# Trunk with top-2-of-8 experts: the expert order computed ahead of the first gather, the last norm's squares ahead of the overflow jump, the last normalise and its stores in column halves

## The chip, the core and the metric

The kernel runs on one core of one Trainium2 chip. TensorE multiplies into PSUM, VectorE (DVE in the rows) and ScalarE (ACT) work between PSUM and SBUF, GpSimd (POOL) builds masks and loads a few small tensors, SyncE (SP) issues nearly all transfers. Each engine takes its own instructions in their order and waits at semaphores for the others. The metric is the device time of one execution in microseconds; lower is better.

## What is computed

A two-layer trunk over 256 frames of width 1024, all in float32. Layer 0 has a spatial-gating and a gated-DeltaNet mixer and a dense SwiGLU. Layer 1 has stick-breaking attention and then the part that the change touches: a router picks two of eight experts for each frame, and every expert is a SwiGLU of inner width 2816. At the end stands one RMSNorm.

```python
def moe_swiglu(xn, w_router, w1, w3, w2):
    logits = (xf @ w_router).astype(jnp.float32)
    vals, idx = lax.top_k(logits, TOP_K)
    gates = jax.nn.softmax(vals, axis=-1)
    combine = jnp.sum(jax.nn.one_hot(idx, N_EXPERTS, dtype=jnp.float32) * gates[..., None], axis=1)
    y = jnp.zeros_like(xf)
    for e in range(N_EXPERTS):
        y = y + combine[:, e:e + 1].astype(xf.dtype) * swiglu(xf, w1[e], w3[e], w2[e])
...
    return rmsnorm(h, final_norm)
```

## The kernel before

The frames lie in two tiles of 128 (index `t`); `h` [128, 2, 1024] is the residual. The line numbers here and in the rows are those of the kernel before.

**Experts.** Expert 0 comes first; the other seven are taken in an order that is found while the kernel runs, by how many frames each got. Slots 0, 2, 4, 6 of that order are "big": their frames (up to 128) are multiplied with weights that are split in a high part (`all_hi`, ScalarE, L883) and a low part (`low`, VectorE, L1904), three matmuls for each product (L620 to L622). Slots 1, 3, 5, 7 are "small": up to 64 frames, full float32 matmuls straight from the loaded weights (L1717 up, L1738 down). What doesn't fit those capacities goes to "overflow items", a loop behind the eight slots that is jumped over when there are none (`n_more` is 0).

**Steps and pieces.** The matmuls of the experts are a list `STEPS`: phase up 0 (slot 0, first half of the inner width, 16 steps of 9 matmuls), up 1 (slot 1, 16 steps), down 0, up 2 (second half of slot 0), down 1, and so on, always two phases of a big slot around those of small ones. The weights come in `PIECES` of 704 KB (up) or 1 MB (down) into one ring in SBUF, `room`. `place_pieces` gives each piece its place and what must have been used before it may be overwritten. Pieces 0 to 15 are those of up 0 and are loaded before the router has decided anything. Pieces 16 to 19 (slot 1) take places that the dense layers' last units held, and piece 20 + k takes a place that step k of up 0 has used. SP issues the pieces in their order (L695) and, ahead of piece 16, waits for `order_ready` and reads the expert's number from `order_i` (L702).

**Router and order on VectorE.** After the top-2 (L2211 to L2228) VectorE writes the table `nat` (place, gate and count for each expert), then `sel_p` (L2239), with which TensorE gathers slot 0's frames (L1661), then `sel_w` (L2246, `places_back(0)`), which is needed for slot 0's way back much later. It splits the gathered frames (`xg_lo`, L2322), and the order is worked out between the splits of up 0: `compare_counts` (L2272 to L2276) at step 0, `rank_experts` (L2280 to L2283) at step 1, `order_table` (L2288 to L2292) at step 2, whose last instruction casts the order into `order_i`.

**The end.** The last slot's result goes back by four matmul groups (L1698), and VectorE adds each to `h` (L2369, four instructions: two column halves of tile 0, then two of tile 1). Each engine then reads `n_more` from `item_i` (TENSOR_LOAD) and jumps over the overflow loop. Behind its jump VectorE raises `h_ready` (drain, L2479), ScalarE loads the exp and ln table (L1195) and does the last norm's squares, ln and exp for each tile (L846 to L848, `inverse_rms(4)`), VectorE multiplies (L1876, one instruction of 1024 columns for each tile), and SP stores each tile with one transfer of 512 KB (L727).

## Time and profile before

| what | value |
|---|---|
| time, median of 3 runs | 1207.49 us (1205.4 to 1207.52) |
| time of the profiled execution | 1207.14 us, of which its span is 1205.3 us |
| TensorE busy | 1149.9 us (95%) |
| VectorE busy | 669.2 us (56%) |
| ScalarE busy | 562.7 us (47%) |
| GpSimd busy | 49.6 us (4%) |
| mean granted TensorE clock | 0.988 |
| transfers | 351.08 MB, mean 291 GB/s |

The span is the time from the first to the last instruction; 1.84 us lie around it. Of the chain of work that ended last, 88% is TensorE. The experts' part begins at about 519 us of the span and its last matmul ends at 1193.66 us; the eight experts hold 276.8 MB of weights.

### The profile page before, as it was taken

To read this page: it belongs to the slowest core of one execution; us is meant where nothing else is said; L and a number is where in the kernel's file an instruction comes from. 1 tells how busy PE (TensorE), PEld (TensorE's weight loads), DVE (VectorE), ACT (ScalarE), POOL (GpSimd) and SP (SyncE) were. 2 spreads that over 40 slices of the span, in tenths; PEclk is the share of its full clock that TensorE was granted. 3 is DMA by queue.
4 is the path that set the end of the run, shared out by engine and by line. 5 is a ranking of instruction groups with operands and counts; after the bars stand their busy time and mean duration, and the time that the engine had idled before them with its cause. 6 is when DMAs were issued, how large, how long until landed. Compare 5 with 4: busy or idle time off the path is not lost.

```text
span 1205.3 us, 16293 instructions
## 1 busy us (share of the span) xinstructions
PE 1149.9 (95%) x6555; PEld 852.7 (71%) x6555; DVE 669.2 (56%) x740; ACT 562.7 (47%) x642; POOL 49.6 (4%) x93
## 2 busy tenths in 40 slices
PE   5989899999999999899999999999999999999995
PEld 5979778888879976685486688648658468387351
DVE  4875664544455523582384788427578058574143
ACT  4772355344444476452363677226447056263131
POOL 8010000000000022000000000000000000000000
PEclk9999999999999999999999999999999999999998
DMA  9632059755325822139999999999999999999992
GB/s 319 184 116 72 29 169 369 238 175 187 128 70 177 330 74 72 66 139 416 413 415 410 413 415 412 400 414 414 411 414 415 415 412 412 413 413 415 413 407 78
DMA packets 116737, 351.08 MB, mean 291 GB/s; under 512 B 8136, under 2 KB 55280, under 8 KB 116656
## 3 DMA queue, kind: packets, MB, share of 16 engines
q1 hardware_dynamic: 115552, 347.11, 74.8%
q0 software_dynamic: 1104, 2.86, 0.8%
q8 instruction: 54, 0.88, 0.3%
q14 instruction: 27, 0.22, 0.1%
HBM read 348.89 MB, written 1.05 MB: 290 GB/s over the span
## 4 chain that ended last, share of the span: by engine, by line
PE 88%; DVE 4%; ACT 2%; DMA 2%; POOL 2%; issue 1%; POOLq 0%; DVEq 0%; ACTq 0%
PE ps L620 20%; PE ps L621 19%; PE ps L622 19%; PE ps L1717 11%; PE ps L1738 7%; PE ps L1661 3%; DMA room<-in_o_moe_w_dram 2%; PE ps L1673 1%; PE ps L1370 1%; DVE low L1904 1%; POOL level L741 1%; PE ps L1578 1%; PE ps L1590 1%; DMA gam<-in_e_sgu_w_dram 1%; PE ps L1698 1%
## 5 line engine op out<-in xcount | busy, mean ns | idle before, releaser
L1904 DVE TENSOR_TENSOR low<-room,all_hi 128x1408 fp32r<-128x1408 f32 (+1 forms) x216 | 308.0, 1458 | 202.6 <-ACT all_hi L883 202.0
L883 ACT ACTIVATE all_hi<-room 128x1408 fp32r<-128x1408 f32 (+1 forms) x216 | 265.3, 1255 | 258.6 <-DMA room<-in_o_moe_w_dram 177.4
L1717 PE MATMUL ps<-room,xg_raw 128*64 128x512 f32 (+1 forms) x768 | 152.5, 558 | 0.0
L620 PE MATMUL ps<-all_hi,xg_hi 128*128 128x512 f32 (+1 forms) x384 | 144.8, 377 | 2.0 <-DVE low L1904 1.0
L621 PE MATMUL ps<-low,xg_hi 128*128 128x512 f32 (+1 forms) x384 | 144.6, 376 | 0.0
L622 PE MATMUL ps<-all_hi,xg_lo 128*128 128x512 f32 (+1 forms) x384 | 144.0, 375 | 0.0
L620 PE MATMUL ps<-all_hi,x_hi 128*128 128x512 f32 (+1 forms) x336 | 125.1, 372 | 5.1 <-ACT xn L972 2.4
L621 PE MATMUL ps<-dense_lo,x_hi 128*128 128x512 f32 (+1 forms) x336 | 122.8, 366 | 0.0
L622 PE MATMUL ps<-all_hi,x_lo 128*128 128x512 f32 (+1 forms) x336 | 122.5, 365 | 0.0
L1717 PEld LDWEIGHTS ps<-room,xg_raw 128*64 128x64 f32 x768 | 54.6, 137 | 95.5 <-issue 95.4
L1897 DVE TENSOR_TENSOR dense_lo<-slots_a,all_hi 128x2048 fp32r<-128x2048 f32 x40 | 91.4, 2290 | 47.5 <-ACT all_hi L876 47.5
L876 ACT ACTIVATE all_hi<-slots_a 128x2048 fp32r<-128x2048 f32 x40 | 76.7, 1918 | 40.7 <-PE ps L622 37.1
L620 PE MATMUL ps<-x_hi,all_hi 128*128 128x256 f32 x288 | 83.0, 288 | 4.4 <-DVE x_lo L1890 3.4
L1738 PE MATMUL ps<-room,m_raw 128*64 128x512 f32 x352 | 83.2, 610 | 2.3 <-DVE y_lo L2359 2.3
L620 PEld LDWEIGHTS ps<-all_hi,xg_hi 128*128 128x128 f32 x384 | 72.1, 188 | 16.9 <-issue 3.5
L1897 DVE TENSOR_TENSOR dense_lo<-slots_c,all_hi 128x2048 fp32r<-128x2048 f32 x25 | 57.3, 2293 | 46.6 <-ACT all_hi L876 46.5
L621 PE MATMUL ps<-x_lo,all_hi 128*128 128x256 f32 x288 | 81.8, 284 | 0.0
L622 PE MATMUL ps<-x_hi,dense_lo 128*128 128x256 f32 x288 | 81.2, 282 | 0.0
L622 PEld LDWEIGHTS ps<-all_hi,xg_lo 128*128 128x128 f32 x384 | 72.1, 188 | 11.5
L621 PEld LDWEIGHTS ps<-low,xg_hi 128*128 128x128 f32 x384 | 72.1, 188 | 11.4
L620 PEld LDWEIGHTS ps<-all_hi,x_hi 128*128 128x128 f32 x336 | 64.1, 191 | 18.6 <-issue 5.5
L620 PE MATMUL ps<-all_hi,m_hi 128*128 128x512 f32 x176 | 71.6, 407 | 2.2 <-DVE m_lo L2342 2.2
(363 smaller groups left out, 1566.9 us busy)
## 6 DMA issues: line engine op xcount, KB each, us to landing
room<-in_o_moe_w_dram SPq DMA_DIRECT2D x256, 704.0 KB, 15.6
room<-in_o_moe_w_dram SPq DMA_DIRECT2D x80, 1024.0 KB, 18.2
slots_c<-in_e_ffn_w_dram SPq DMA_DIRECT2D x36, 512.0 KB, 6.8
slots_a<-in_e_ffn_w_dram SPq DMA_DIRECT2D x30, 512.0 KB, 5.3
slots_a<-in_e_w_in_dram SPq DMA_DIRECT2D x24, 512.0 KB, 8.7
slots_a<-in_o_w_qkv_dram SPq DMA_DIRECT2D x18, 512.0 KB, 4.5
room<-in_o_moe_w_dram SPq DMA_DIRECT2D x16, 512.0 KB, 17.1
slots_a<-in_e_w_out_dram SPq DMA_DIRECT2D x8, 512.0 KB, 4.0
```

Source lines behind the costliest of these rows:

```text
L620: pe.matmul(o, a_hi, b_hi, start=first, stop=False)
L621: pe.matmul(o, a_hi, b_lo, start=False, stop=False)
L622: return pe.matmul(o, a_lo, b_hi, start=False, stop=last)
L741: after(pool.affine_select(out=t, in_=t, pattern=pattern, compare_op=op, fill=fill, base=base, channel_multiplier=cm))
L876: act.activation(w_hi[i % SPLITS][:, :], ring[slot][:, :], ACT.Copy).then_inc(hi_done, 1)
L883: act.activation(unit_hi(st), raw_of(v, off, st.size), ACT.Copy).then_inc(hi_done, 1)
L1370: last = mm(ps[rows, bank, m * CH:(m + 1) * CH], a(u, rows), b(u, rows), start=True, stop=True)
L1661: last = mm(ps[:, gather_bank(q, c // 4), at:at + n], xn[:, t, c * P:(c + 1) * P], sel_p[:, t, 0:n], start=(t == 0), stop=(t == TILES - 1))
L1717: last = mm(ps[a * SMALL:(a + 1) * SMALL, o + b, 0:n], xg_raw[:, c, :], raw[a][:, c0:c0 + n], start=(c == 0), stop=(c == DC - 1))
L1738: last = mm(ps[hf * SMALL:(hf + 1) * SMALL, y_bank(st.q), :], m_raw[st.n % 2][:, j, st.a * SMALL:(st.a + 1) * SMALL], raw[:, hf * 512:(hf ...
L1897: tt(w_lo[i % SPLITS][:, :], ring[slot][:, :], w_hi[i % SPLITS][:, :].bitcast(F32), ALU.subtract).then_inc(lo_done, 1)
L1904: tt(unit_lo(st), raw_of(v, off, st.size), unit_hi(st).bitcast(F32), ALU.subtract).then_inc(lo_done, 1)
```

## The change

- `order_experts` is new: it works out only the order (one row of 49 products, a sum, a cast into `order_i`) and raises `order_ready`. `compare_counts`, `rank_experts` and `order_experts` now stand in front of `gathered(0)`, and `places_back(0)` behind it. `order_table` stays at step 2 without its cast.
- The last norm's squares, ln and exp (`last_rms`) stand on ScalarE in front of its read of `n_more` and its jump; they wait for the adds of each tile (`scat_added`) and write the squares into a tile of their own. If there are overflow items, they are done again behind them (`more_added`, `more_normed`).
- VectorE reads `n_more` ahead of the last slot's four adds, jumps behind them, has no drain on the path without items, and normalises each tile in two column halves; SP stores each half (256 KB) as it is ready.

```diff
+                act.wait_ge(scat_added, 4 * (NE - 1) + 2 * (t + 1))
+                last_rms(t, rinv_ready)
...
             with act.If(n_more > 0):
...
-            act.preload_act_table_set(EXP_LN)
-            inverse_rms(4)
...
-            places_back(0)
...
-                vec.tensor_copy(order_i[0:1, :], tab[0:1, 6, 0:NE]).then_inc(order_ready, 1)
...
+            def order_experts():
+
+                after(tt(ids_moved, nat[0:1, 6, 1:NE].unsqueeze(1).to_broadcast([1, R7, R7]), rank4[0:1, 3], ALU.mult))
+                after(vec.tensor_reduce(ids_order[:, 1:NE], ids_moved, AX.X, ALU.add))
+                vec.tensor_copy(order_i[0:1, 1:NE], ids_order[:, 1:NE]).then_inc(order_ready, 1)
+
+            compare_counts()
+            rank_experts()
+            order_experts()
             gathered(0)
+            places_back(0)
...
-                    if st.j == 0:
-                        compare_counts()
-                    if st.j == 1:
-                        rank_experts()
...
             finished(NE - 1)
+            vec.wait_ge(items_ready, 1)
+            n_more = vec.value_load(item_i[0:1, 0, 0:1], min_val=0, max_val=7)
             add_out(NE - 1)
...
-            vec.wait_ge(items_ready, 1)
-            n_more = vec.value_load(item_i[0:1, 0, 0:1], min_val=0, max_val=7)
             with vec.If(n_more > 0):
...
-            vec.wait_ge(items_ready, 1)
-            vec.drain().then_inc(h_ready, 2 * TILES)
+                vec.drain().then_inc(more_added, 1)
+                vec.wait_ge(more_normed, TILES)
+            vec.wait_ge(ld_gain, 48)
             for t in range(TILES):
-                normalise(4, t)
+                vec.wait_ge(rinv_ready, TILES * 4 + t + 1)
+                for hf in range(2):
+                    cs = slice(hf * 512, (hf + 1) * 512)
+                    stt(xn[:, t, cs], h[:, t, cs], stat[:, 4, 4 + t:5 + t], gain[:, 0, cs], ALU.mult, ALU.mult)\
+                        .then_inc(out_ready, 1)
```

**VectorE at the first gather, before.** `low8960` is the low part of up 0's step 2 and `low10368` that of step 3; a name's first number is its place in `room`.

```order
L2246 TENSOR_SCALAR sel_w_56<-iota,nat_50 128x128 [waits vec_own]
...
L2322 TENSOR_TENSOR xg_lo_62<-ps,xg_hi_61 128x512 [waits xgh_ready] x2
L1904 TENSOR_TENSOR low8960_7327<-room_49,all_hi 128x1408 [waits hi_done]
L2272 TENSOR_TENSOR router_tmp_58<-nat_50 128x49 [waits counts_read]
...
L1904 TENSOR_TENSOR low10368_7338<-room_49,all_hi 128x1408 [waits hi_done,vec_own]
...
L2283 TENSOR_TENSOR router_tmp_58<-router_tmp_58 128x49 [waits vec_own]
...
L2290 TENSOR_REDUCE tab_51<-router_tmp_58 128x56 [waits vec_own]
L2291 COPY tab_51<-nat_50 128x8
L2292 CAST order_i_54<-tab_51 1x8 [waits vec_own]
L1904 TENSOR_TENSOR low14592_7371<-room_49,all_hi 128x1408 [waits hi_done]
```

**The same place after the change.**

```order
L2301 TENSOR_TENSOR router_tmp_58<-router_tmp_58 128x49 [waits vec_own]
L2390 TENSOR_TENSOR router_tmp_58<-nat_50,router_tmp_58 1x49 [waits vec_own]
L2391 TENSOR_REDUCE router_tmp_58<-router_tmp_58 1x7 [waits vec_own]
L2392 CAST order_i_54<-router_tmp_58 1x7 [waits vec_own]
L2339 TENSOR_TENSOR xg_lo_63<-ps,xg_hi_62 128x512 [waits xgh_ready] x2
L2266 TENSOR_SCALAR sel_w_56<-iota,nat_50 128x128 x2
L1924 TENSOR_TENSOR low8960_7343<-room_49,all_hi 128x1408 [waits hi_done]
...
L2308 TENSOR_REDUCE tab_51<-router_tmp_58 128x8x7 [waits vec_own]
L2309 COPY tab_51<-nat_50 128x8
L1924 TENSOR_TENSOR low14592_7387<-room_49,all_hi 128x1408 [waits hi_done,vec_own]
```

The order's cast now stands ahead of the wait for the gathered frames instead of behind the fourth split of up 0, `sel_w` stands behind that wait, and the nine instructions of `compare_counts` and `rank_experts` are gone from between the splits.

**ScalarE behind the last slot's result, after the change** (before, the read of `item_i` stood right behind the copy to `y_small`, and the table load and the squares, which waited for `h_ready`, behind the jump).

```order
L1156 ACTIVATE y_small_75<-ps 64x512 [waits raw_used]
L1186 ACT_TABLE_LOAD
L1182 ACTIVATE squares_59,stat<-h 128x1024 [waits scat_added]
L1183 ACTIVATE stat<-stat,const 128x1 [waits act_own]
L1184 ACTIVATE stat<-stat 128x1 [waits act_own]
L1182 ACTIVATE squares_59,stat<-h 128x1024 [waits scat_added]
...
L1204 TENSOR_LOAD item_i_53 [waits items_ready]
L1204 ISA x2
L1205 COMPARE_AND_BRANCH
```

The six activations no longer have a jump, of ScalarE's or of VectorE's, ahead of them.

## Rows read from the trace of the kernel before

**Rows 1.** Waits of SP's queue, 519 to 600 us: total us, times, longest.

```profile
SPq L702 <- DVE order_i L2292: 34.1, 1, 34.1
```

**Rows 2.** Busy us of each engine by stretch, granted clock, DMA share, GB/s.

```profile
554.40:594.20 39.80, 39.79 (x204) 14.63 (x203) 3.73 (x6) 2.87 (x4) 0.00 (x0) 1.00 1.02 415
594.20:603.30 9.10, 6.91 (x30) 5.69 (x30) 9.10 (x11) 8.52 (x12) 0.00 (x0) 0.81 1.02 410
...
770.00:780.00 10.00, 10.00 (x50) 4.22 (x51) 0.00 (x0) 0.00 (x0) 0.00 (x0) 1.00 0.98 375
780.00:1160.00 380.00, 378.92 (x1862) 243.74 (x1859) 207.58 (x196) 169.83 (x175) 0.00 (x0) 1.00 1.02 413
```

**Rows 3.** Timeline of VectorE around the first gather: start us, us, instruction.

```profile
514.94 0.60 DVE L2246 TENSOR_SCALAR sel_w<-iota,nat 128x128 f32<-128x128 f32 x2
517.79 0.69 DVE L2322 TENSOR_TENSOR xg_lo<-ps,xg_hi 128x512 fp32r<-128x512 f32 x1 [2.25 <-ACT xg_hi L1120]
...
520.54 1.62 DVE L1904 TENSOR_TENSOR low<-room,all_hi 128x1408 fp32r<-128x1408 f32 x1
522.07 0.20 DVE L2272 TENSOR_TENSOR router_tmp<-nat 128x49 f32<-128x49 f32 x1
...
525.85 0.20 DVE L2280 TENSOR_TENSOR router_tmp<-router_tmp 128x49 f32<-128x49 f32 x1
...
526.57 0.21 DVE L2283 TENSOR_TENSOR router_tmp<-router_tmp 128x49 f32<-128x49 f32 x1
...
528.36 0.56 DVE L2288 TENSOR_TENSOR router_tmp<-nat,router_tmp 128x392 f32<-128x392 f32 x1
...
529.63 0.16 DVE L2292 CAST order_i<-tab 1x8 int32<-1x8 f32 x1
```

**Rows 4.** Timeline of TensorE, the first matmul of up 0's step 6.

```profile
531.37 0.50 PE L620 MATMUL ps<-all_hi,xg_hi 128*128 128x512 f32 x1 [0.57 <-DVE low L1904]
```

**Rows 5.** The chain that ended last, from up 1 to down 0.

```profile
572.35 20.05 DMA room<-in_o_moe_w_dram
...
592.42 1.07 ACT all_hi L883
...
596.39 0.80 PE ps L620
597.19 0.43 PE ps L621
...
599.75 0.26 PE ps L621
```

**Rows 6.** Timeline of ScalarE ahead of slot 6's down phase.

```profile
1139.22 2.01 ACT L883 ACTIVATE all_hi<-room 128x1024 fp32r<-128x1024 f32 x2 [41.20 <-DMA room<-in_o_moe_w_dram]
```

**Rows 7.** The chain over the experts' part, at that down phase.

```profile
1143.91 0.43 PE ps L620
```

**Rows 8.** The chain at the end; DVEq is VectorE's sequencer.

```profile
1192.82 1.39 DVE h L2369 x2
...
1194.61 0.07 DVEq L2467
...
1197.46 0.02 DVEq L2478
...
1197.57 1.16 ACT xn L846 x2
...
1199.08 0.20 ACT stat L848
...
1200.92 1.28 DVE xn L1876
```

**Rows 9.** ScalarE's read of `item_i`: ns, first and last start.

```profile
L1187 ACTq TENSOR_LOAD <-item_i x1: 462/462/462, 1190.8 to 1190.8; - x1
```

**Rows 10.** Timeline of ScalarE behind that read.

```profile
1192.03 1.28 ACT L1195 ACT_TABLE_LOAD   x1 [0.61 <-issue]
```

**Rows 11.** DMA share in 40 slices of 0.1 us, 1202 to 1206 us.

```profile
DMA  9899899820499899899999930000000000000000
```

More of the change, by code:

```diff
@@ L421, in trunk @@
         router_tmp = over(gain_at + 4 * D)[0]("router_tmp", [P, D])
+        squares = over(gain_at + 4 * D)[0]("squares", [P, D])
         y_hi = over(gain_at + 4 * D)[0]("y_hi", [SLOTS, D], F32R)
@@ L1172, in _, with last_rms @@
             finished(NE - 1)
+            def last_rms(t, ready):
+                after(act.activation(squares[:, :], h[:, t, :], ACT.Square, accum_out=stat[:, 4, t:t + 1]))
+                after(act.activation(stat[:, 4, 2 + t:3 + t], stat[:, 4, t:t + 1], ACT.Ln, scale=1.0 / D, bias=eps_col))
+                act.activation(stat[:, 4, 4 + t:5 + t], stat[:, 4, 2 + t:3 + t], ACT.Exp, scale=-0.5).then_inc(ready, 1)
+            act.preload_act_table_set(EXP_LN)
+            for t in range(TILES):
+                act.wait_ge(scat_added, 4 * (NE - 1) + 2 * (t + 1))
+                last_rms(t, rinv_ready)
             def evac_y(n):
@@ L1189, in _ @@
                 used(act, A_ITEM - 1)
+                act.preload_act_table(ACT.Silu)
                 with act.Fori(0, n_more) as it:
```

27 lines of the change are left out of this document (18 added, 9 removed).

## Prediction

> **What bounds the kernel now.** I read the waits of SP's queue first. For the order of the experts it stands still for 34.1 us [rows 1], until the cast that ends at 529.79 us [rows 3]; after that the transfers never rest. The busy times by stretch come next: from there on the DMA share is 1.01 to 1.03 at some 413 GB/s, and TensorE is busy all the time too, 378.92 of 380 us between 780 and 1160 us [rows 2]. Two full resources don't bind alike, so the waits decide. TensorE has nearly no idle time behind 603 us, while the transfers run short once: 375 instead of 413 GB/s between 770 and 780 us, 0.9 us of their time, where the next piece waited for a place that TensorE had yet to use. So the experts' part is bound by TensorE, and the transfers are a close second. Then I looked for the places where TensorE does wait. There are three that the change could touch. At step 6 of up 0 it waits 0.57 us for VectorE's low part [rows 4]. Between up 1 (busy until 594.2 us, 39.79 of 39.80 us [rows 2]) and down 0 (first matmul at 596.39 us [rows 5]) it waits 2.2 us, and the chain goes back over ScalarE's split to a transfer that lands at 592.4 us: data that came late because the order did. And at the end everything hangs on a string of single steps [rows 8].
>
> **The change, part by part, at the start.** `compare_counts` takes the place that `sel_w` had at 514.94 us and lasts 0.6 us (its five instructions begin at 522.07 us and are through when the next one can start), `rank_experts` 0.95 us (four, first and last in rows 3), `order_experts` three links of the same kind, 0.65 us. The order is ready at 514.94 + 0.6 + 0.95 + 0.65 = 517.15 us, 12.6 us before 529.79 us. That is 0.6 us ahead of VectorE's wait for the gathered frames, which ends at 517.79 us, so this cover hides it; each 0.1 us beyond would delay the gather's low parts and up 0 by as much.
>
> What it costs later: `sel_w` (0.6 us) now stands between `xg_lo` and the low part of step 2, which began at 520.54 us. That one would begin at 521.1 us and end at 522.7 us; TensorE starts step 0 at about 519.0 us by my estimate, a step being 4224 columns at the 0.24 us for 512 that the matmuls take at the full clock (0.26 us with its tail in rows 5), 1.94 us, so step 2 starts at 522.9 us. Cost between 0 and 0.3 us, taken as 0. Before step 6's low part VectorE loses 0.6 + 0.95 + 0.2 us (the cast) and gains 0.6 us of `sel_w`: it is 1.1 us earlier, more than the wait of 0.57 us. Gain 0.6 us (0 to 0.7).
>
> Do the transfers really come earlier? Pieces 16 to 19 need nothing of up 0; they are 4 x 0.721 MB / 413 GB/s = 7.0 us of transfer. Piece 20 + k needs step k, and the steps free one each 1.94 us where a piece takes 1.75 us, and stop for slot 1's gather. So the lead when up 0 ends lies between 7.0 and 12.6 us, and I take 9. Up 1 frees two pieces a step and holds nobody up. The piece of the 592.4 us needs to come 2.2 + 0.6 us earlier and comes 9 earlier; down 0's splits and `m_lo` then lie wholly beside up 1's matmuls, in which VectorE and ScalarE are nearly idle (3.73 and 2.87 us of 39.80 [rows 2]). The wait of 2.2 us goes.
>
> With it goes its echo. Behind the wait the granted clock of the stretch is 0.81 [rows 2]: matmuls take 0.43 us, the lower of the two levels (1.2 GHz), from 596.39 to 599.75 us, and then 0.26 us [rows 5]. 3.36 us of work at half speed are 1.6 us lost (1.5 to 1.7). Without the gap TensorE runs on at 2.4 GHz. Sum of the start: 0.6 + 2.2 + 1.6 = 4.4 us.
>
> **Is it kept until the end?** TensorE has no slack behind it, so a shift stays a shift if its data come as early. At 770 us the transfers already wait for TensorE; with 9 us of lead against 4.4 us they wait there longer, and from that place both run as before, only 4.4 us earlier. How thin that is: ahead of slot 6's down phase the data come at 1139.22 us [rows 6]; with one high part (1.0 us) and one low part (1.2 us) they are ready at 1141.5 us, for matmuls that start at 1143.91 us [rows 7]. The margin is 2.4 us.
>
> **The end.** Tile 0's adds are through at 1194.21 us; its squares began at 1197.57 us and would begin at 1194.26 us. Squares to exp took 1.71 us for tile 0 and 3.31 us for both [rows 8], so the scales are there at 1195.97 and 1197.57 us; the adds of tile 1 end at 1195.53 us, in time for the second squares. The table load, 1.28 us [rows 10], falls between the copy and the adds.
>
> VectorE's jump stays behind the adds. Its branch stood at 1194.61 us and its next instruction at 1197.46 us [rows 8]: 2.85 us. The read in front of it, 0.46 us for ScalarE [rows 9] and some 0.3 us around it, is now hidden ahead of the adds, so VectorE gets through at 1196.65 us. The change moves the read, not the jump: this and no longer ScalarE would be late next. Bounds: a jump that must wait for the last add to end, 1195.53 + 2.85 = 1198.4 us; or one as cheap as ScalarE's, whose read, jump and all cost 0.61 us of idle time [rows 10], and then the scales decide. Four halves of 1.28 / 2 = 0.65 us end at 1199.25 us instead of 1202.20 us: gain 2.95 us (1.2 to 3.3). I take the middle one since it is this engine's own jump.
>
> The Trainium skill ("Runtime: NRT & Kernel Launch", Instruction fetch mechanics) says that a taken branch whose target isn't in the pages already fetched stalls for a fetch. That fits VectorE's dear jump and ScalarE's cheap one; since VectorE's jump spans the same loop as before, it would stay dear by that rule too, and a lucky page would give the 3.3 us.
>
> The last store's data take 1.4 us, from slice 10 to slice 23 [rows 11]; a half takes 0.65 us less, if rows of 2 KB move as fast as rows of 4 KB (0 to 0.65 us; taken 0.65). Sum of the end: 3.6 us (1.2 to 4.0).
>
> **Sum.** 4.4 + 3.6 = 8.0 us: 1207.14 - 8.0 = 1199.1 us, 0.35 us more against the median of the runs. I say 1199.3 us; the bounds alone give 1198.6 to 1202.1 us.
>
> **Rivals.** *The lead is taken back*: the transfers don't keep up behind 780 us, and TensorE keeps only its margin of 2.4 us. For it: a DMA share of 1.02 throughout. Against it: the gap at 770 us. 1207.14 - 2.4 - 3.6 = 1201.1 us. *The transfers are the bound after all*: then all 12.6 us come through, 1191 us; against it stands TensorE without waits. *The order brings nothing*: the second expert's pieces wait for room, not for the order; only the end is left, 1203.5 us. The 34.1 us of rows 1 speak against it.
>
> *The stores run one after another.* Between the last multiply's end (1202.20 us) and the end of the span lie 3.1 us, 1.4 of them data, so 1.7 us are fixed. Four halves in a row are 4 x 2.35 = 9.4 us from 1197.3 us, 5.1 us more than in the forecast: 1204.2 us. The second store's packets follow the first's within 0.2 us [rows 11], which speaks against it. The Trainium skill ("DMA: Bandwidth & Descriptors", Rules for kernel authors) asks for 1 MB or more in a transfer, which is the rule against the halves.
>
> *Slower:* transfers that are ahead get issued one by one as places come free, and each then shows its fixed time. With 1.7 us on each of up 0's 16 pieces they lose 27 us, are 14 us late instead of 12.6 early, and TensorE waits for about that long: 1217 us. It decides where fewer than two transfers are under way. When they did run short, at 770 us, it cost 0.9 us.
>
> **Chances.** Forecast 0.70, lead taken back 0.13, order brings nothing 0.06, transfers the bound 0.05, stores in a row 0.03, slower 0.03. A measurement of this kernel can tell about 0.2% (2.4 us) from no change. All but the last are faster by more than that; with the stores' case close to it I give 0.94 faster, 0.03 within, 0.03 slower. The range holds the first two cases, the bounds and the spread of 2.1 us between the runs of before: 1196.8 to 1203.0 us.
>
> **What would show it.** The cast into `order_i` near 517 us and the transfers 12.6 us earlier; no wait at step 6; down 0's first matmul right behind up 1, at a granted clock of 1.00; the last expert matmul 4.4 us earlier; the first squares right behind tile 0's adds; VectorE idle until 2.4 us behind them. I am wrong if TensorE waits for data behind 603 us, or if VectorE's jump lasts otherwise.

## The result, and where the 7 us came from

The changed kernel takes 1200.44 us (median of 4 runs, 1199.14 to 1201.01), the kernel before in the same rounds 1207.51 us (4 runs, 1205.4 to 1208.23). The ratio is 0.9943, 95% interval 0.9926 to 0.996: 7.1 us less, 8.0 were forecast, and the forecast of 1199.3 us is 1.1 us short. The profiled execution took 1201.01 us with a span of 1199.3 us; against the profiled execution of before (1207.14 and 1205.3 us) that is 6.0 us of span, and these are accounted for below, from the front of the program to its end. Lines behind the first few hundred stand 4 to 28 lines further down than before: L625 to L627 are the three matmuls of a split product, L1737 and L1758 the small slots' up and down matmuls.

**The order.** Timeline of VectorE in the changed kernel (start us, us, instruction), to hold against [rows 3]:

```profile
516.78 0.16 DVE L2392 CAST order_i<-router_tmp 1x7 int32<-1x7 f32 x1
517.58 0.69 DVE L2339 TENSOR_TENSOR xg_lo<-ps,xg_hi 128x512 fp32r<-128x512 f32 x1 [0.64 <-ACT xg_hi L1126]
```

and the waits of SP's queue there (total us, times, longest), to hold against [rows 1]:

```profile
SPq L707 <- DVE order_i L2392: 21.4, 1, 21.4
```

The cast ends at 516.94 us (forecast 517.15) and SP waits 12.7 us less (forecast 12.6). The idle 0.64 us in front of `xg_lo` is still there: the cover held, the gather's low part waited for ScalarE and not for the order.

**The busy times by stretch** (length, busy us of TensorE's matmuls and weight loads, VectorE, ScalarE, GpSimd, granted clock, DMA share, GB/s), to hold against [rows 2]:

```profile
554.40:592.90 38.50, 38.50 (x201) 14.19 (x195) 7.17 (x9) 7.55 (x11) 0.00 (x0) 1.00 1.01 404
592.90:602.00 9.10, 9.10 (x46) 7.47 (x45) 8.14 (x9) 7.07 (x10) 0.00 (x0) 1.00 1.02 415
750.00:760.00 10.00, 10.00 (x64) 8.81 (x63) 9.90 (x14) 5.25 (x9) 0.00 (x0) 1.00 0.89 347
760.00:770.00 10.00, 10.00 (x47) 6.62 (x47) 1.61 (x3) 0.00 (x0) 0.00 (x0) 1.00 0.88 304
770.00:780.00 10.00, 10.00 (x54) 3.61 (x52) 0.00 (x0) 0.00 (x0) 0.00 (x0) 1.00 1.00 391
780.00:1160.00 380.00, 375.64 (x1841) 242.59 (x1839) 208.98 (x200) 170.28 (x177) 0.00 (x0) 1.00 1.02 413
```

TensorE works without a break around 593 us, where it had waited 2.2 us, and the granted clock is 1.00 in place of 0.81. The chain at the same place (start us, us, what; compare [rows 5]):

```profile
571.73 21.41 PE ps L1737 x108
593.14 0.43 PE ps L625
593.57 0.23 PE ps L626
```

No transfer is in it any more: down 0 comes right behind up 1. Its first matmul starts 3.3 us earlier than in [rows 5]; 0.2 us of that lay already ahead of up 0, 0.8 are the wait of step 6 [rows 4] and what hung on it, 2.3 the wait ahead of down 0. The matmuls then run at 0.23 us where those of [rows 5] ran at 0.43 until 599.75 us, so that at slot 0's turn the lead is 4.8 us. TensorE keeps nearly all of it for 540 us (4.5 us at slot 6's down phase).

**Where the lead was spent.** The transfers give their 12.7 us back in two stretches. The first lies beside the end of up 0 (the same columns as above; the changed kernel, then the kernel before):

```profile
540.00:570.00 30.00, 30.00 (x149) 17.60 (x149) 8.52 (x10) 7.01 (x9) 0.00 (x0) 1.00 0.94 353
```

```profile
540.00:570.00 30.00, 30.00 (x154) 18.30 (x155) 9.50 (x11) 7.10 (x9) 0.00 (x0) 1.00 1.02 417
```

353 GB/s instead of 417 for 30 us are 4.6 us of lead: up 0's steps free the places no faster, as the forecast said when it took 9 us for the lead behind up 0. Between 750 and 780 us they run at 347, 304 and 391 GB/s instead of 413: (66 + 109 + 22) GB/s times 10 us over 413 GB/s, 4.8 us more, of which the kernel before loses 0.9 too. That was forecast for 770 us (the transfers wait for places that TensorE has yet to use); it began 20 us earlier and took more, because the lead was greater. 12.7 - 4.6 - 3.9 = 4.2 us are left, about TensorE's own lead. Behind it the margin was to be 2.4 us at slot 6's down phase. In this execution it was not there. ScalarE's timeline (start us, us, instruction), to hold against [rows 6], and the waits of TensorE:

```profile
1136.85 2.01 ACT L889 ACTIVATE all_hi<-room 128x1024 fp32r<-128x1024 f32 x2 [43.55 <-DMA room<-in_o_moe_w_dram]
1139.40 2.02 ACT L889 ACTIVATE all_hi<-room 128x1024 fp32r<-128x1024 f32 x2 [0.55 <-DMA room<-in_o_moe_w_dram]
...
PE ps L1693 <- DVE u_act L2349: 0.9, 1, 0.9
```

In the kernel before the first pair of high parts starts at 1139.22 us [rows 6] and the second at

```profile
1141.78 2.01 ACT L883 ACTIVATE all_hi<-room 128x1024 fp32r<-128x1024 f32 x2 [0.55 <-DMA room<-in_o_moe_w_dram]
```

The data of both pairs come 2.4 us earlier in the changed kernel, while TensorE comes 4.5 us earlier: 2.1 us of the 2.4 us of margin are gone. ScalarE's split of the late piece then stands in front of `u_act`, and TensorE waits for that (0.9 us, and some tenths around it). 3.5 us of lead are left when the last slot's matmuls end.

**The end.** The chain of the changed kernel (start us, us, what), to hold against [rows 8]:

```profile
1189.25 0.97 DVE h L2386 x2
...
1190.56 1.40 DVE h L2386 x2
1191.96 1.14 issue
1193.11 0.02 DVEq L2505
...
1193.18 1.42 DVE xn L2508 x2
```

and ScalarE beside it:

```profile
1190.68 1.06 ACT L1182 ACTIVATE squares<-h 128x1024 f32<-128x1024 f32 x1 [1.53 <-DVE h L2386]
...
1192.19 0.20 ACT L1184 ACTIVATE stat<-stat 128x1 f32<-128x1 f32 x1
```

The first scale is there at 1192.39 us, but VectorE starts to multiply at 1193.18 us. Its own jump is what is late next, as forecast: the instruction behind the jump comes 1.15 us behind the last add, where 1196.65 against 1195.53 us, that is 1.12, was worked out. From the first add to the end of the span it takes 10.06 us, in the kernel before 12.48 us: 2.4 us gained. 3.5 and 2.4 us make the 6.0 us of the span. The forecast had 4.4 and 3.6.

### The profile page after: what moved, and what is told of

It reads as the page before. It is cut to its first block, busy times and chain, and to the rows that moved or that the text cites. A ratio compares the mean times of both kernels' runs of the same rounds, so it can differ in the third digit from the quotient of the medians.

```text
span 1199.3 us, 16296 instructions
## 1 busy us (share of the span) xinstructions
PE 1148.1 (96%) x6555; PEld 851.9 (71%) x6555; DVE 669.4 (56%) x744; ACT 561.9 (47%) x642; POOL 49.5 (4%) x93
## 4 chain that ended last, share of the span: by engine, by line
PE 89%; DVE 4%; DMA 2%; ACT 2%; POOL 2%; issue 1%; POOLq 0%; DVEq 0%; ACTq 0%; SPq 0%
PE ps L625 20%; PE ps L626 20%; PE ps L627 20%; PE ps L1737 11%; PE ps L1758 7%; PE ps L1681 3%; DMA room<-in_o_moe_w_dram 2%; PE ps L1693 1%; PE ps L1390 1%; POOL level L747 1%; PE ps L1598 1%; PE ps L1610 1%; DMA gam<-in_e_sgu_w_dram 1%; PE ps L1718 1%; PE ps L1715 1%
## 5 line engine op out<-in xcount | busy, mean ns | idle before, releaser
L1737 PE MATMUL ps<-room,xg_raw 128*64 128x512 f32 (+1 forms) x768 | 152.5, 558 | 0.0
L625 PE MATMUL ps<-all_hi,xg_hi 128*128 128x512 f32 (+1 forms) x384 | 145.0, 378 | 1.4 <-DVE y_small L2378 1.0
L627 PE MATMUL ps<-all_hi,xg_lo 128*128 128x512 f32 (+1 forms) x384 | 144.2, 375 | 0.0
L625 PE MATMUL ps<-all_hi,x_hi 128*128 128x512 f32 (+1 forms) x336 | 125.2, 373 | 5.1 <-ACT xn L978 2.4
L627 PE MATMUL ps<-all_hi,x_lo 128*128 128x512 f32 (+1 forms) x336 | 122.6, 365 | 0.0
L1737 PEld LDWEIGHTS ps<-room,xg_raw 128*64 128x64 f32 x768 | 54.6, 137 | 95.5 <-issue 95.3
L625 PE MATMUL ps<-x_hi,all_hi 128*128 128x256 f32 x288 | 83.0, 288 | 4.5 <-DVE x_lo L1910 3.5
L1758 PE MATMUL ps<-room,m_raw 128*64 128x512 f32 x352 | 83.1, 610 | 2.3 <-DVE y_lo L2376 2.3
L625 PEld LDWEIGHTS ps<-all_hi,xg_hi 128*128 128x128 f32 x384 | 72.2, 188 | 16.0 <-issue 3.5
L627 PE MATMUL ps<-x_hi,dense_lo 128*128 128x256 f32 x288 | 81.2, 282 | 0.0
L627 PEld LDWEIGHTS ps<-all_hi,xg_lo 128*128 128x128 f32 x384 | 72.2, 188 | 11.6
L625 PEld LDWEIGHTS ps<-all_hi,x_hi 128*128 128x128 f32 x336 | 64.2, 191 | 18.6 <-issue 5.5
L627 PEld LDWEIGHTS ps<-all_hi,x_lo 128*128 128x128 f32 x336 | 64.0, 190 | 10.0
```

The costliest lines, as they stand in the source:

```text
L625: pe.matmul(o, a_hi, b_hi, start=first, stop=False)
L627: return pe.matmul(o, a_lo, b_hi, start=False, stop=last)
L1737: last = mm(ps[a * SMALL:(a + 1) * SMALL, o + b, 0:n], xg_raw[:, c, :], raw[a][:, c0:c0 + n], start=(c == 0), stop=(c == DC - 1))
L1758: last = mm(ps[hf * SMALL:(hf + 1) * SMALL, y_bank(st.q), :], m_raw[st.n % 2][:, j, st.a * SMALL:(st.a + 1) * SMALL], raw[:, hf * 512:(hf ...
```

## The experiments

All twelve kernels in order, each with the kernel before timed in the same rounds:

| label | what | median us (range) | ratio to before, 95% |
|---|---|---|---|
| e1 | early order alone | 1202.08 (1199.48 to 1204.18) | 0.9961, 0.9947 to 0.9974 |
| e2 | new end alone | 1203.96 (1202.5 to 1208.12) | 0.998, 0.9971 to 0.9988 |
| e3 | whole tiles in multiply and store | 1198.84 (1197.25 to 1201.65) | 0.9938, 0.9925 to 0.9951 |
| e4 | halves multiplied, whole tiles stored | 1200.47 (1197.48 to 1202.61) | 0.9943, 0.993 to 0.9956 |
| e5 | cast at step 0 | 1200.58 (1198.27 to 1201.3) | 0.9939, 0.9917 to 0.996 |
| e6 | cast at step 2 | 1201.19 (1199.87 to 1201.49) | 0.9946, 0.9926 to 0.9965 |
| e7 | VectorE's read behind the adds again | 1202.14 (1199.18 to 1202.62) | 0.9947, 0.9929 to 0.9966 |
| e8 | multiplies ahead of the jump | 1198.91 (1198.25 to 1199.82) | 0.9929, 0.9909 to 0.9948 |
| e9 | only the last of the four stores | 1198.7 (1197.65 to 1199.02) | 0.9928, 0.9913 to 0.9943 |
| e10 | extra matmuls in two waits | 1199.12 (1197.26 to 1200.61) | 0.9935, 0.9921 to 0.9949 |
| e11 | e8, e10 and a shorter wait | 1198.1 (1196.67 to 1199.32) | 0.9923, 0.9909 to 0.9936 |
| e12 | e11 with fewer extra matmuls | 1199.7 (1196.53 to 1200.07) | 0.9929, 0.9916 to 0.9942 |

The executions of one kernel differ by 1.4 to 5.6 us. Between the profiled executions of different kernels a large part of the difference arises in the dense layers, which no kernel here touches: the router's first matmul starts anywhere between 498.89 (e3) and 502.88 us (e4). TensorE's rows for it, of e3 and e4 (500.67 us in the kernel before):

```profile
498.89 2.20 PE L1232 MATMUL ps<-ident,h 128*128 128x128 f32 x16
```

```profile
502.88 2.20 PE L1232 MATMUL ps<-ident,h 128*128 128x128 f32 x16
```

So the profiled executions are compared in three stages counted from there (us): from that matmul to up 0's first, from this to the last slot's first add, and from the add to the end of the span.

| | router to up 0 | up 0 to first add | first add to end | sum |
|---|---|---|---|---|
| before | 18.35 | 673.80 | 12.48 | 704.6 |
| changed | 18.32 | 670.45 | 10.06 | 698.8 |
| e1 | 18.05 | 669.35 | 12.45 | 699.8 |
| e2 | 18.24 | 673.67 | 9.69 | 701.6 |
| e3 | 18.61 | 667.57 | 10.13 | 696.3 |
| e4 | 18.24 | 669.28 | 10.30 | 697.8 |
| e5 | 18.26 | 669.21 | 9.80 | 697.3 |
| e6 | 18.30 | 669.39 | 9.98 | 697.7 |
| e7 | 18.28 | 669.32 | 10.49 | 698.1 |
| e8 | 18.51 | 669.30 | 9.89 | 697.7 |
| e9 | 18.46 | 669.26 | 9.18 | 696.9 |
| e10 | 18.17 | 668.72 | 9.90 | 696.8 |
| e11 | 18.13 | 667.77 | 9.79 | 695.7 |
| e12 | 17.85 | 667.80 | 9.90 | 695.6 |

### e1 and e2: the two parts apart

Early order alone, against the kernel before:

```diff
+            compare_counts()
+            rank_experts()
+            order_experts()
             gathered(0)
+            places_back(0)
...
-                    if st.j == 0:
-                        compare_counts()
-                    if st.j == 1:
-                        rank_experts()
```

> The kernel before with the order part alone (order ahead of the first gather, sel_w behind it); its end is as before. Theory (two parts that add up): TensorE stands 4.7 us earlier from 600 to 1139 us, as in the trace of after, and loses about 1.2 us in front of the last big slot's first turn, where the transfers have no lead left: last expert matmul 3.4 to 3.6 us earlier, whole time 3.5 us under the kernel before. Rival 1 (the loss of 1.2 us belongs to the other part of the change or to that one execution): 4.7 us under before. Rival 2 (the transfers bind, whatever TensorE does): the same 1.2 us, but a gain that varies by over 1 us from run to run.

New end alone, which is the changed kernel with the order undone:

```diff
+                vec.tensor_copy(order_i[0:1, :], tab[0:1, 6, 0:NE]).then_inc(order_ready, 1)
...
-            compare_counts()
-            rank_experts()
-            order_experts()
             gathered(0)
-            places_back(0)
...
+                    if st.j == 0:
+                        compare_counts()
+                    if st.j == 1:
+                        rank_experts()
```

> The kernel before with the end alone (squares ahead of the jump, VectorE's read ahead of the adds, last normalise and stores in column halves); the order as before. Theory: the span ends 2.4 us earlier, as the trace of after shows behind the last scatter (6.0 us in all less 3.57 us at the scatter), so 2.4 us under before, and TensorE's part is unchanged to within 0.3 us. Rival (the prediction's sum for the end was right and the trace of after caught a slow last store): 3.6 us under before.

e1 is 0.39% faster, 4.7 us (3.1 to 6.4); e2 0.2%, 2.4 us (1.4 to 3.5). Together 7.1 us, what the change brought: the parts add up. The stages say the same: e1 gains 4.45 us between up 0 and the first add and nothing behind it, e2 2.8 us behind it and nothing before. By these two the order's 4.4 us were sized well, the end's 3.6 us were not. e2 has its waits of TensorE between 519 and 603 us back, nearly those of before:

```profile
PE ps L625 <- DVE m_lo L2362: 2.5, 1, 2.5
PE ps L625 <- DVE low L1924: 0.6, 1, 0.6
```

and yet its clock didn't fall behind them: the chain shows down 0's first matmul at 595.12 us and the others at 0.23 us,

```profile
595.12 0.50 PE ps L625
595.84 0.23 PE ps L627
```

so the 1.6 us that the forecast called an echo of the wait hang on the execution, and don't follow from the wait each time. From down 0's first matmul to up 2's it took 18.07 us in the kernel before and 16.55 in e2. e2 gave 1.1 us of it back behind up 2: 530.5 us from up 2 to slot 6's down phase, where the kernel before took 529.4. The waits of TensorE behind 603 us show where:

```profile
PE ps L625 <- DVE y_small L2381: 2.0, 1, 2.0
```

In the kernel before this wait is 1.0 us, and so it is in every kernel but e2 and e6. It ends at 669.71 us in e2, and the chain behind it goes from a transfer that lands at 665.8 us over ScalarE's split and VectorE's low part to `y_small`. So with the order late, most of what TensorE doesn't lose to its clock at down 0 it waits for 70 us later, because the data are no earlier.

### e3 and e4: what the halves bring

Whole tiles, against the changed kernel:

```diff
-            for m in range(2 * TILES):
-                t, cs = m // 2, slice((m % 2) * 512, (m % 2 + 1) * 512)
-                sp.wait_ge(out_ready, m + 1)
-                sp.dma_start(out[0, t * P:(t + 1) * P, cs], xn[:, t, cs]).then_inc(out_sem, 16)
+            for t in range(TILES):
+                sp.wait_ge(out_ready, t + 1)
+                sp.dma_start(out[0, t * P:(t + 1) * P, :], xn[:, t, :]).then_inc(out_sem, 16)
...
-                for hf in range(2):
-                    cs = slice(hf * 512, (hf + 1) * 512)
-                    stt(xn[:, t, cs], h[:, t, cs], stat[:, 4, 4 + t:5 + t], gain[:, 0, cs], ALU.mult, ALU.mult)\
-                        .then_inc(out_ready, 1)
+                stt(xn[:, t, :], h[:, t, :], stat[:, 4, 4 + t:5 + t], gain[:, 0, :], ALU.mult, ALU.mult)\
+                    .then_inc(out_ready, 1)
```

> After, with only the halves undone: each tile normalised by one instruction and stored by one transfer of 512 KB. The prediction put 0.65 us on the smaller last store, so undoing it would cost 0.65 us (and nothing on VectorE). Theory now: rows of 2 KB move no faster for each row than the prediction assumed away; four instructions of 0.69 us take 2.74 us where two took 2.8, and the last store of the trace of after ended 3.4 us behind the last multiply instead of 3.1 us before. So the halves bring nothing: this kernel is the same as after within 0.3 us, perhaps 0.3 us faster.

e4 leaves the multiplies in halves and stores whole tiles:

```diff
-            for m in range(2 * TILES):
...
+            for t in range(TILES):
+                sp.wait_ge(out_ready, 2 * t + 2)
+                sp.dma_start(out[0, t * P:(t + 1) * P, :], xn[:, t, :]).then_inc(out_sem, 16)
```

> After, with the multiplies in halves but one store of 512 KB with rows of 4 KB for each tile, when both halves are done. If rows of 2 KB are what makes the last stores slow, this equals e3_whole_tiles and lies 0 to 0.3 us under after; if it is the starting of the store when half a tile is done that counts (the prediction's 0.65 us), it is 0.65 us slower than after.

The times of all three can't be told apart (0.9938, 0.9943 and 0.9943). Since all of it happens behind the last adds, the traces say more: from the first add to the end of the span e3 takes 10.13 us, e4 10.30, the changed kernel 10.06. The halves are worth 0.1 to 0.2 us, forecast 0.65. The other kernels with halves and the same jump (e2, e5, e6, e10) lie between 9.69 and 9.98 us, which makes it 0.6 us at the most. e3's two whole multiplies take less than four halves:

```profile
1188.92 2.48 DVE L2505 SCALAR_TENSOR_TENSOR xn<-h,stat,gain 128x1024 f32<-128x1024 f32 x2 [1.13 <-ACT stat L1183]
```

2.48 us against 2.74 us, so 0.26 us of what a shorter last store brings go back. The Trainium skill ("DMA: Bandwidth & Descriptors", Rules for kernel authors) asks for transfers of 1 MB or more; here four of 256 KB cost nothing against two of 512 KB, and the rival of stores that run one after another is out: e4 isn't faster. (That e3 shows 667.57 us in the middle stage has nothing to do with its stores; see e10.)

### e5 and e6: how much lead is needed

The cast alone is moved back, to step 0 of up 0 (e5) or to step 2 (e6); nothing else changes:

```diff
-                vec.tensor_copy(order_i[0:1, 1:NE], ids_order[:, 1:NE]).then_inc(order_ready, 1)
...
                 if st.kind == "up" and st.n == 0:
+                    if st.j == 0:
+                        vec.tensor_copy(order_i[0:1, 1:NE], ids_order[:, 1:NE]).then_inc(order_ready, 1)
```

> After, with only the cast into order_i (the last of the order's instructions) moved behind the split of up 0's step 2, so that SP gets the order about 5 us later than in after (near 522 us instead of 517 us), and everything else in its place. Theory (the transfers need only 2.9 us of lead at down 0; the rest of the 12.6 us is given back in places where they wait for room): same time as after, down 0 right behind up 1 at the full clock, and less time in which the transfers run short between 540 and 560 us. Rival (each us of earlier transfers is worth one): about 5 us slower than after.

> After, with the cast at step 2, where the kernel before had it: SP gets the order near 528 us. Theory: VectorE's relief at step 6 stays (0.6 to 0.8 us), but TensorE waits again in front of down 0, a bit less than the 2.2 us of the kernel before plus the 0.8 us by which it is earlier, and loses about 1.5 us by the lower clock behind it: 3.5 us slower than after over that place. Rival (the wait went by the reordering on VectorE): same as after.

SP's waits for the order are 21.4 us in the changed kernel, and here 26.9 (e5) and 31.7 us (e6):

```profile
SPq L707 <- DVE order_i L2405: 31.7, 1, 31.7
```

5.5 us less lead cost nothing: TensorE has no wait between 519 and 603 us in e5, and the transfers run short in one of the two stretches only, and less there (353 and 347 GB/s in the changed kernel):

```profile
540.00:570.00 30.00, 30.00 (x157) 18.65 (x157) 9.77 (x11) 7.21 (x10) 0.00 (x0) 1.00 1.02 416
750.00:780.00 30.00, 30.00 (x162) 19.82 (x162) 13.05 (x17) 6.79 (x10) 0.00 (x0) 1.00 0.95 371
```

Less lead, fewer transfers that wait for room; in e6 it is 415 and 410 GB/s, next to no shortage. With 10.3 us less lead (e6) one wait is back,

```profile
PE ps L625 <- DVE m_lo L2359: 1.1, 1, 1.1
```

and the clock stays at its higher level. From up 0 to the first add e6 takes as long as e5, but only because its clock was better behind down 7 (27.1 us to the last matmul group, 28.8 in e5; below): up to there it is 1.9 us behind e5, 1.1 by this wait and 0.7 by the one for `y_small` at 670 us (1.7 against 1.0 us), the same that e2 has. So of the 12.7 us that the order comes earlier, TensorE uses only the first 3 to 4 at down 0: e2's 2.5 us and e6's 1.1 us of the same wait lie 2.3 us of lead apart, and e6's TensorE comes 0.8 us earlier by step 6, so that it reaches zero with 1.1 us of lead more (an estimate: 2.3 + 1.1 = 3.4 us). The rest is given back from 540 and from 750 us on. The rival by which the transfers are the bound (all 12.6 us would come through) is out.

### e7 and e8: the jump at the end

e7 puts VectorE's read of `n_more` behind the adds again:

```diff
             finished(NE - 1)
-            vec.wait_ge(items_ready, 1)
-            n_more = vec.value_load(item_i[0:1, 0, 0:1], min_val=0, max_val=7)
             add_out(NE - 1)
...
+            vec.wait_ge(items_ready, 1)
+            n_more = vec.value_load(item_i[0:1, 0, 0:1], min_val=0, max_val=7)
             with vec.If(n_more > 0):
```

> After, with VectorE's read of the number of overflow items put back behind the last adds, next to the jump. Theory (read and jump are one string on VectorE's sequencer and bound the first multiply): the first multiply starts 0.8 us later, 1.9 instead of 1.15 us behind the last add, and the time is 0.8 us longer. Rival (the jump waits for the last add to end): no difference.

```profile
1194.71 2.74 DVE L2508 SCALAR_TENSOR_TENSOR xn<-h,stat,gain 128x512 f32<-128x512 f32 x4 [2.07 <-ACT stat L1184]
```

The multiplies start 2.07 us behind the last add, in the changed kernel 1.22: the read costs 0.85 us there, where 0.46 and some 0.3 were read. The end of the span, though, moves by 0.4 us only against the changed kernel (10.49 and 10.06 from the first add); e2, e5, e6 and e10, with the same end, took 9.69 to 9.98 us, so that 0.4 to 0.8 us is what these traces can say.

e8 does the opposite: the normalisation stands ahead of the jump, in a tile `final` of its own.

```diff
+            vec.wait_ge(ld_gain, 48)
+            last_normalise(out_ready, rinv_ready, TILES * 4)
             with vec.If(n_more > 0):
+                vec.wait_ge(out_ready, 2 * TILES)
```

> After, with the last normalise in front of VectorE's jump too, written to a tile of its own and done again behind the overflow items if there are any. Theory (the jump bounds the first multiply, the scale of tile 0 is there 0.8 us earlier, and behind the first multiply 1 MB of stores takes some 6 us whatever is in halves): the first multiply starts right behind the scale, 3.2 us behind the first add instead of 3.95 us, and the time is 0.7 to 0.8 us under after. Rival (the scale of tile 1 bounds the end): under 0.3 us.

```profile
1191.47 2.94 DVE L2499 SCALAR_TENSOR_TENSOR final<-h,stat,gain 128x512 f32<-128x512 f32 x4 [0.54 <-ACT stat L1186]
```

and ScalarE's last step there, the second scale:

```profile
1192.77 0.20 ACT L1186 ACTIVATE stat<-stat 128x1 f32<-128x1 f32 x1
```

Now the scales decide, 0.54 us behind the last add, and the first multiply comes 0.7 us earlier. But from the first add to the end of the span it is 9.89 us, a gain of 0.17. A part of the 0.7 us is lost on VectorE itself: the second scale comes at 1192.97 us, the third multiply waits for it (2.94 us for the four instead of 2.74), and the last multiply ends 0.5 us earlier than in the changed kernel, counted from the first add. The rival of the expectation, that tile 1's scale bounds the end, has this much for it. The other 0.3 us are not paid out at the end either, so something else stands there too.

### e9: the queue in front of the last store

That something should be the stores themselves: VectorE makes a half in 0.69 us, and 256 KB at 373 GB/s take 0.7 us too. e9 makes all four halves and stores only the last one; three quarters of the output are left out.

```diff
                 sp.wait_ge(out_ready, m + 1)
-                sp.dma_start(out[0, t * P:(t + 1) * P, cs], xn[:, t, cs]).then_inc(out_sem, 16)
+                if m == 2 * TILES - 1:
+                    sp.dma_start(out[0, t * P:(t + 1) * P, cs], xn[:, t, cs]).then_inc(out_sem, 16)
```

> After, with three of the four stores of the result left out: only tile 1's second half (256 KB) is stored. The prediction's term: a last store of 256 KB ends 2.45 us behind the last multiply; in the trace of after it is 3.4 us. Theory (the last store is small, but its data queue behind those of the three stores ahead of it, since the multiplies make 256 KB in 0.69 us and the transfers move them in about as much): without them the span ends 2.4 to 2.6 us behind the last multiply, 0.8 to 1.0 us under after. Rival (rows of 2 KB are slow in themselves, or the receipt of a store lasts longer): still over 3 us behind it.

Stretches of 0.5 us, first of the changed kernel, whose multiplies end at 1195.92 us,

```profile
1195.00:1195.50 0.50, 0.00 (x0) 0.00 (x0) 0.50 (x2) 0.00 (x0) 0.00 (x0) 0.50 1.00 373
1195.50:1196.00 0.50, 0.00 (x0) 0.00 (x0) 0.42 (x1) 0.00 (x0) 0.00 (x0) 0.50 1.07 377
1196.00:1196.50 0.50, 0.00 (x0) 0.00 (x0) 0.00 (x0) 0.00 (x0) 0.00 (x0) 0.50 0.98 369
1196.50:1197.00 0.50, 0.00 (x0) 0.00 (x0) 0.00 (x0) 0.00 (x0) 0.00 (x0) 0.50 0.83 303
1197.00:1197.50 0.50, 0.00 (x0) 0.00 (x0) 0.00 (x0) 0.00 (x0) 0.00 (x0) 0.50 0.82 315
1197.50:1198.00 0.50, 0.00 (x0) 0.00 (x0) 0.00 (x0) 0.00 (x0) 0.00 (x0) 0.50 0.61 230
1198.00:1198.50 0.50, 0.00 (x0) 0.00 (x0) 0.00 (x0) 0.00 (x0) 0.00 (x0) 0.50 0.05 20
```

then of e9, whose multiplies end at 1194.74 us:

```profile
1195.50:1196.00 0.50, 0.00 (x0) 0.00 (x0) 0.00 (x0) 0.00 (x0) 0.00 (x0) 0.50 0.59 225
1196.00:1196.50 0.50, 0.00 (x0) 0.00 (x0) 0.00 (x0) 0.00 (x0) 0.00 (x0) 0.50 0.80 299
```

In e9 the span ends 2.56 us behind the last multiply, in the changed kernel 3.38 us. The forecast's 3.1 - 0.65 = 2.45 us is right for a store that has the queues for itself; the three in front of it cost the other 0.8 us. The six profiled kernels with these four stores and this jump (the changed one, e2, e5 to e7 and e10) lie between 2.95 and 3.4 us, so the cost is 0.4 to 0.8 us, and the changed kernel's trace is at the dear end.

The bytes alone don't explain it. The first packet of the changed kernel's stores starts at 1194.83 us; at 373 GB/s the megabyte would be through at 1197.6 us, and a last store that is alone would be through then too (its data end 1.78 us behind the last multiply in e9). What costs is that the rate falls to 303, 315, 230 and 20 GB/s. The transfer engines also finish apart: the 16 small packets that close a store lie within 0.15 us of each other in e9, but 0.7 us apart for the last store of the changed kernel (0.5 to 0.8 us in the six). Why they drift apart wasn't found. In e8 the megabyte takes 3.9 us from its first packet to its last, in the six 3.3 to 3.8 us; the rest of what VectorE wins there goes into this. In the kernel before, whose two stores are 0.2 us apart, it takes 2.95 us, and the span ends 3.1 us behind the last multiply: no later than with halves.

### e10 to e12: waits and the clock behind them

In two places TensorE waits and then works at the lower of its two levels (1.2 GHz) for some us. Behind the router's wait of 3.4 us it does so in every kernel up to e9: the first gather takes 5.6 to 6.2 us (in e3, e8 and e9 the first small matmuls behind the wait still run at the higher level, 0.37 us against 0.57, and the gather doesn't). Behind the wait for `y_lo` (2.3 us, in down 7) it depends on the execution: from down 7 to the last matmul group it takes 28.8 us in nine of the profiled kernels up to e9, and 27.15 us in e3 and e6. TensorE's granted clock in that stretch is the third number from the end, in the changed kernel and in e3:

```profile
1160.00:1165.00 5.00, 5.00 (x20) 1.56 (x16) 0.00 (x0) 0.00 (x0) 0.00 (x0) 0.74 1.03 410
```

```profile
1160.00:1165.00 5.00, 5.00 (x23) 1.74 (x20) 1.19 (x3) 0.00 (x0) 0.00 (x0) 1.00 1.03 410
```

e10 puts matmuls into these waits whose results nobody uses:

```diff
+            for k in range(6):
+                mm(ps[:, 1, :], ident[:, :], h[:, 0, 0:512], start=True, stop=True)
             pe.wait_ge(sel_ready, 1)
...
                 if q == 0:
+                    mm(ps[:, 1, :], ident[:, :], h[:, 0, 0:512], start=True, stop=True)
...
+                    if n == PHASES - 1:
+                        for k in range(4):
+                            mm(ps[:, 3, :], ident[:, :], xn[:, 0, 0:512], start=True, stop=True)
```

> After, with 7 matmuls more (512 columns, their results are used by nobody) in TensorE's waits around the router and 4 in its wait in front of the last slot's down phase. In the runs so far the stretch from the first gather to up 0 lasted 2.8 to 5.6 us and that from the last down phase to the last scatter 27.15 or 28.8 us, each with another granted clock. Theory (TensorE falls to 1.2 GHz in these two waits in some executions and not in others, and that is most of the spread of the runs): with TensorE kept at work there the first stretch lasts about 2.8 us and the last 27.2 us in the profile, the time is 2 to 3 us under after and the runs lie closer together. Rival (the clock falls for another reason): both stretches as before, time as after or up to 1 us longer.

The stretch of the gather, of the changed kernel and of e10 (the granted clock is the third number from the end):

```profile
511.00:517.00 6.00, 5.49 (x26) 5.43 (x27) 5.41 (x27) 1.81 (x4) 0.00 (x0) 0.50 0.00 0
```

```profile
511.00:517.00 6.00, 6.00 (x41) 4.69 (x40) 4.70 (x23) 2.36 (x4) 0.00 (x0) 1.00 0.00 0
```

and the matmuls there, again of the changed kernel and of e10:

```profile
513.16 5.88 PE L1681 MATMUL ps<-sel_p,xn 128*128 128x128 f32 x32 [0.51 <-DVE sel_p L2259]
```

```profile
509.76 2.74 PE L1665 MATMUL ps<-h,ident 128*128 128x512 f32 x6
512.34 0.28 PE L1668 MATMUL ps<-r,before 128*128 128x8 f32 x2
...
514.31 3.73 PE L1684 MATMUL ps<-sel_p,xn 128*128 128x128 f32 x32
```

The gather runs in 3.73 instead of 5.88 us. Almost all of these 2.15 us is given back in front of it: the router's small matmuls could have started at about 510.5 us, as in the changed kernel, and stood behind the extra ones until 512.34 us. From the router to up 0 it is 18.17 us, 0.15 less. At down 7 the clock stays at 1.00, but the eight instructions last 3.59 us in a wait of 2.3. The ratio of 0.9935 lies inside the interval of the changed kernel.

e11 joins e8, e10 (three matmuls at the second place) and, at the last scatter, a wait that asks for one half of `y` less:

```diff
-                        pe.wait_ge(y_act, y_count(before_it))
-                        pe.wait_ge(y_vec, y_count(before_it))
+                        pe.wait_ge(y_act, y_count(before_it) - first_half)
+                        pe.wait_ge(y_vec, y_count(before_it) - first_half)
```

> After with e8_norm_ahead's end, e10_filler's matmuls (3 instead of 4 at the second place), and the last slot's down phase waiting only for the first half of the slot ahead of it (the half whose bank it writes). Theory: e10_filler's gain, 0.6 us for the shorter wait and 0 to 0.5 us for the end: 3 to 4 us under after, 10 us under before. Rival (the transfers have no more lead to give at the last big slot, so what TensorE gains at the first gather is waited for there): 1.5 to 2 us under after.

At 0.9923 it has the lowest ratio of all, 9.3 us below before (7.7 to 11.0), against the 7.1 us of the changed kernel; the two intervals overlap. The stages show from where: 667.77 us from up 0 to the first add, 1.5 us less than e4, e5 and e7 to e9, which all agree within 0.14 us. But e3, without any extra matmul, shows 667.57 us when its clock doesn't fall at down 7. So what e11 adds there is what an execution with the better clock has anyway.

e12 is e11 with four extra matmuls for six, and none directly ahead of the gather:

```diff
-            for k in range(6):
+            for k in range(4):
                 mm(ps[:, 1, :], ident[:, :], h[:, 0, 0:512], start=True, stop=True)
...
-                    mm(ps[:, 1, :], ident[:, :], h[:, 0, 0:512], start=True, stop=True)
                     pe.wait_ge(xn_ready, 2 * TILES)
```

> The kernel of e11 with fewer extra matmuls at the router: four instead of six ahead of the small ones, and none directly ahead of the first gather. In e10 the twelve instructions of the six ran from 507.08 to 512.34 us, while TensorE had waited only until 510.4 us there without them: they kept the clock and cost 1.9 us. Four of them last 3.5 us and end when the wait would end anyway. Theory (the clock of this stretch is what the spread and the loss come from): the gather runs at the higher level, 3.7 instead of 5.9 us, and up 0 begins 1.5 us earlier than in e10 measured from the small matmuls' data: the ratio to before falls from 0.9923 to 0.991, about 1196.6 us. Rival A: the idle 0.5 us ahead of the gather is enough to bring the lower level back; then the gather takes 5.9 us again and the time is that of e8, 1198.9 us or more. Rival B: the gather isn't what the later parts wait for (a wait of 0.6 us ahead of up 0 stood in e10), so that the wait grows by what the gather gains: 1198.1 us as in e11.

Its ratio of 0.9929 can't be told from e11's. The profiled execution shows rival A: without the extra matmul a wait of 1.39 us stands ahead of the gather, and the gather takes 5.44 us.

```profile
515.30 5.44 PE L1685 MATMUL ps<-sel_p,xn 128*128 128x128 f32 x32 [1.39 <-DVE sel_p L2267]
```

From the router to up 0 it takes 17.85 us, 0.3 us less than e11: what the four extra matmuls no longer delay is lost again in the gather. Its six runs fall in two groups, 1196.53 and 1196.54 us and 1199.66 to 1200.07 us. The profiled one is of the slower group and had its router 2.1 us later than e10's, so the groups may as well come from the dense layers; that stays open.

## Why the prediction was right, and where it was not

- *The order 12.6 us earlier and hidden by `xg_lo`'s wait*: right, 12.7 us, and the idle 0.64 us is still in front of `xg_lo`.
- *Step 6, 0.6 us, and the wait ahead of down 0, 2.2 us*: right, 0.8 and 2.3 us. The lead of 9 us behind up 0 was right too: 12.7 - 4.6 = 8.1 us. The reading that held was to ask for each wait of TensorE which chain ended it, and whether that chain went back to the order.
- *The echo in the clock, 1.6 us*: it came in the profiled pair (18.07 to 16.56 us), but e2 has the wait without it. As a term it is a chance, not a certainty, and e2 shows that it isn't worth 1.6 us by itself: 1.0 us of it was waited for again at 669 us, because the data were no earlier. That e1's 4.7 us come so near the forecast 4.4 says how large the sum is, not how large this term is.
- *"From that place both run as before", margin 2.4 us*: the claim fails in the profiled execution, which lost 1.2 us at slot 6, where the data came 2.4 us earlier and not 4.5. By the prediction's own sign, a wait for data behind 603 us, it was wrong there. It was no property of the change: e1 and e3 to e8 show no wait for `u_act` there and keep their lead. Why this execution's data were 2.1 us short wasn't found. TensorE was also less free of waits behind 603 us than the prediction read: the kernel before waits 2.3 us for `y_lo`, 1.6 us in three waits for `sel_w` and 1.9 us in two for `y_small`, and the changed kernel has them all unchanged. The rival "the lead is taken back" would take 2 us each time, and e1's 4.7 us speak against it.
- *Which transfers would wait*: right in kind, at 540 to 570 and at 750 to 780 us. e5 shows that almost half of the lead was never needed.
- *The end, first multiply*: right. 1.15 us from the last add to the instruction behind VectorE's jump (1.12 worked out), four multiplies 2.74 us (2.6). The Trainium skill ("Runtime: NRT & Kernel Launch", Instruction fetch mechanics) lets a taken branch out of the fetched pages stall for a fetch, and gives no price; the 2.85 us of [rows 8] were the price here, and the sum made with them came out again. That a fetch is what fills them no run here shows.
- *The end, last store, 0.65 us*: this is the term that failed. It took the last store as alone in the queues. With three stores directly in front of it the last one ends 3.38 us behind the last multiply, where 2.45 were forecast (e9: 2.56 us without the three; 2.95 to 3.4 us in six traces; 3.1 us before). So the term came out between 0.1 us gained and 0.3 us lost. With 0.14 us more in the multiplies this is nearly all of the 1.2 us by which the end fell short: 3.6 forecast, 2.4 measured (2.4 by e2's ratio, 2.8 in its trace).

Both errors, at slot 6 and at the last store, went the same way: in the profiled pair 6.0 of 8.0 us came, by the ratio 7.1; the other profiled kernels with the early order are without the first error. That the sum is so near is in part luck, as the echo counted in full could have been missing in either kernel. Of the rivals, the stores in a row and the order that brings nothing are refuted by e4 and e1, and the slower one by the transfers themselves: with up 0's pieces issued one by one they did run short, 353 GB/s from 540 to 570 us, but that cost 4.6 us of lead and not 27.

## What to carry to other kernels

Ask of a resource that comes earlier how much earlier its user can take it: here 3 to 4 us of 12.7 were used, and the first gap in the transfers told beforehand that the rest would be given back. When a last transfer is cut into pieces that are made as fast as they are moved, don't price the last piece as if it were alone: measure it with the others directly in front of it. When a timeline is compared with another one, pair the same instruction in both, not the one whose time looks alike. And before a term rests on TensorE's clock, look at the same place in a second execution.

## What the runs showed of the hardware that I had not expected

- The same wait brings the lower clock level in one execution and not in the next: behind 2.2 and 2.5 us of idle time at down 0 the matmuls took 0.43 us in the kernel before and 0.23 us in e2; behind 2.3 us at down 7 a phase took 28.8 or 27.15 us. Behind 3.4 us at the router every execution without extra matmuls was slow, 5.6 to 6.2 us for a gather of 3.73 us.
- Where the 4 us between e3 and e4 arise ahead of the router was not looked into beyond the granted clock of the first stretches (1.00 throughout in e3, 0.97 from 50 to 100 us in e4 and in the kernel before), which makes the clock the candidate.
- Four stores directly behind each other have a slow end: the transfers fall to 230 and then 20 GB/s in the last two steps of 0.5 us, and the span ends 0.8 us behind the last packet. The same last store by itself (e9) moves at 299 GB/s until it is through.
- Two multiplies of 1024 columns take 2.48 us, four of 512 take 2.74 us: 0.13 us for each cut.
